# Six 32-byte tiles moved ahead of the weight region in SBUF: every tile of that region, with two gain tiles and a table tile, lies 192 bytes higher

## The reference, cut to what matters

```python
h = rms_norm(x, norm_mix_pre)
z = h @ w_in                                  # 1024 x 1024 @ 1024 x 2816
a = window_attention(rope(aq), rope(ak), av, sink)   # band of +-128, 8 heads of 64
r = retention(rq, rk, rv, rg, ...)            # 4 heads of 128, two directions
x = x + rms_norm(concat(a, r) @ w_out, ...)   # @ 1024 x 1024
q = h2 @ xa_wq;  kv = mn @ xa_wkv             # 256 memory tokens
x = x + rms_norm(softmax(q k') v @ xa_wo, ...)
gate, up = split(h3 @ ffn_w_gu)               # @ 1024 x 5632
x = x + rms_norm((silu(gate) * up) @ ffn_w_down, ...)
```

## Time and profile before

| | |
|---|---|
| median of 3 runs | 1387.6 us (1385.53 to 1387.71) |
| span of the profiled execution, first to last instruction | 1384.9 us |
| TensorE busy | 1364.0 us, 98% of the span, 6644 matmuls |
| weight loads (PEld) busy | 1136.0 us, 82% |
| VectorE, ScalarE, GpSimd busy | 878.7, 671.2, 882.7 us |
| granted clock of TensorE, mean | 1.000 |
| chain that ended last | PE 80%, DVE 8%, ACT 4%, POOL 3%, issue 2%, DMA 2% |

### The profile page before, as it was taken

One profiled execution on the slowest core, in us unless ns is written; L12 is line 12 of the kernel. 1 busy time (PEld: TensorE's weight loads), 2 busy tenths in 40 slices (PEclk: granted clock), 3 DMA queues, 4 the chain that ended last, 5 costly groups with the idle time before them and its releaser, 6 DMA issues.

```text
span 1384.9 us, 18822 instructions
## 1 busy us (share of the span) xinstructions
PE 1364.0 (98%) x6644; PEld 1136.0 (82%) x6644; DVE 878.7 (63%) x1230; ACT 671.2 (48%) x1357; POOL 882.7 (64%) x624
## 2 busy tenths in 40 slices
PE   7999999999999999999999999999999999999998
PEld 7998888767988888888888788888888888878886
DVE  5799997787987788764278732233333334574878
ACT  6432233677686774354386433333333333534454
POOL 1697256335778976512355788777777773799653
PEclk9999999999999999999999999999999999999999
DMA  5676133332028554301535233333333225933354
GB/s 205 208 251 208 53 92 93 106 122 93 1 62 304 182 179 152 101 26 39 190 124 182 88 102 100 107 100 114 114 103 109 97 81 199 355 96 96 115 203 153
DMA packets 137756, 183.56 MB, mean 133 GB/s; under 512 B 10304, under 2 KB 82368, under 8 KB 137664
## 3 DMA queue, kind: packets, MB, share of 16 engines
q1 hardware_dynamic: 135360, 177.25, 38.7%
q10 hardware_dynamic: 2304, 5.13, 1.0%
HBM read 136.98 MB, written 45.35 MB: 132 GB/s over the span
## 4 chain that ended last, share of the span: by engine, by line
PE 80%; DVE 8%; ACT 4%; POOL 3%; issue 2%; DMA 2%; SPq 0%; DVEq 0%; ACTq 0%; POOLq 0%
PE ps L1407 23%; PE ps L1409 23%; PE ps L1408 23%; PE ps L1398 4%; PE ps L1921 2%; PE ps L1619 1%; PE ps L1581 1%; POOL w_lo L1276 1%; DMA raw<-in_xa_wkv_dram 1%; PE ps L1673 1%; ACT tables L2132 1%; DVE x L3807 1%; DMA raw<-o_sums 1%; DVE left_a L3751 1%; DVE yf L3800 1%
## 5 line engine op out<-in xcount | busy, mean ns | idle before, releaser
L1407 PE MATMUL ps<-w_hi,t_hi 128*128 128x512 f32 (+2 forms) x576 | 219.4, 381 | 2.2 <-DVE t_lo L3026 1.2
L1409 PE MATMUL ps<-w_hi,t_lo 128*128 128x512 f32 (+2 forms) x576 | 217.6, 378 | 0.0
L1408 PE MATMUL ps<-w_lo,t_hi 128*128 128x512 f32 (+2 forms) x576 | 217.4, 377 | 0.0
L1138 POOL TENSOR_TENSOR w_lo<-raw,w_hi 128x512 fp32r<-128x512 f32 (+1 forms) x52 | 82.9, 1601 | 95.6 <-ACT w_hi L2185 95.4
L1407 PEld LDWEIGHTS ps<-w_hi,t_hi 128*128 128x128 f32 x576 | 108.2, 188 | 20.3 <-DVE t_lo L3026 1.6
L1409 PEld LDWEIGHTS ps<-w_hi,t_lo 128*128 128x128 f32 x576 | 108.2, 188 | 17.7
L1408 PEld LDWEIGHTS ps<-w_lo,t_hi 128*128 128x128 f32 x576 | 108.3, 188 | 17.1
L1292 POOL TENSOR_TENSOR w_lo<-raw,w_hi 128x512 fp32r<-128x512 f32 x32 | 42.0, 1322 | 96.9 <-ACT w_hi L2663 96.9
L3709 DVE TENSOR_TENSOR ev<-ps,ev 128x512 f32<-128x512 f32 x21 | 14.5, 691 | 135.1 <-PE ps L1409 135.1
L2853 ACT ACTIVATE ev<-ps 128x512 f32<-128x512 f32 x63 | 37.4, 594 | 86.1 <-PE ps L1409 86.1
L2185 ACT ACTIVATE w_hi<-raw 128x512 fp32r<-128x512 f32 (+1 forms) x52 | 31.4, 616 | 97.1 <-PE ps L1409 96.8
(11 more groups left out here) (391 smaller groups left out, 4114.4 us busy)
## 6 DMA issues: line engine op xcount, KB each, us to landing
raw_a<-in_ffn_w_gu_dram SPq DMA_DIRECT2D x44, 256.0 KB, 3.2
raw_b<-in_ffn_w_gu_dram SPq DMA_DIRECT2D x44, 256.0 KB, 3.2
f_rows<-fs SPq DMA_DIRECT2D x44, 256.0 KB, 3.7
gain_b<-f_rows SPq DMA_DIRECT2D x39, 256.0 KB, 2.8
tables<-f_rows SPq DMA_DIRECT2D x38, 256.0 KB, 2.7
f_rows<-fa SPq DMA_DIRECT2D x33, 256.0 KB, 3.5
raw<-in_xa_wo_dram SPq DMA_DIRECT2D x32, 256.0 KB, 2.6
wd_rest<-in_ffn_w_down_dram SPq DMA_DIRECT2D x15, 512.0 KB, 7.3
```

Of the source, the lines that this page charges most:

```text
L1138: nc.gpsimd.tensor_tensor(w_lo[:, k, 0:width], raw[:, k, 0:width], w_hi[:, k, 0:width].bitcast(F32), ALU.subtract).then_inc(w_split, 1)
L1407: nc.tensor.matmul(out, a_hi, b_hi, start=start, stop=False, skip_group_check=onto)
L1408: nc.tensor.matmul(out, a_hi, b_lo, start=False, stop=False, skip_group_check=onto)
L1409: return nc.tensor.matmul(out, a_lo, b_hi, start=False, stop=stop, skip_group_check=onto)
```

## The change

```diff
         dec_t = sb("dec_t", [P, 3, 2 * RH])
 
+        sink_in = sb("sink_in", [P, AH])
+        sink = sb("sink", [P, AH])
+        nsink = sb("nsink", [P, AH])
+        dec = sb("dec", [P, 2 * RH])
+        lg = sb("lg", [P, 2 * RH])
+        cdec = sb("cdec", [P, 2 * RH])
+
         R = overlay(
...
         gain_a = sb("gain_a", [P, D])
         gain_b = sb("gain_b", [P, D])
-        sink_in = sb("sink_in", [P, AH])
-        sink = sb("sink", [P, AH])
-        nsink = sb("nsink", [P, AH])
-        dec = sb("dec", [P, 2 * RH])
-        lg = sb("lg", [P, 2 * RH])
-        cdec = sb("cdec", [P, 2 * RH])
         vpow = sb("vpow", [P, 2 * RH])
```

## The result

The changed kernel takes 1396.56 us (median of 4 runs, 1394.09 to 1397.62), the one before 1387.44 (4 runs, 1385.53 to 1387.71). The ratio is 1.0067, 95% interval 1.0054 to 1.0079: slower by 9 us, where no change was forecast. (The time still lies inside the stated range, in the part that a slower rival had brought in.)

A forecast was written before the change was run, and what follows sets the result against it. TensorE was taken as the bound, busy 1364.0 of 1384.9 us. The terms summed to 0, so the span stayed at 1384.9 us; with the runs' median 2.7 us above, the forecast was 1387.6 us, range 1370 to 1398.

The forecast's parts named there:

- slower rival: TensorE's shifted pairs run at 230.0 ns: 2340 x 3.3 ns = +7.7 us, 1395.3 us; slower had chance 0.26.
- Step (b): TensorE's 2340 matmuls with one operand shifted against the other, 1752 with the stream 64 bytes below, 588 above: price 0.
- faster end: Lower bound on the price of TensorE's shifted matmuls: 2340 x -10.6 ns = -24.8 us.
- slower end: Upper bound for TensorE's shifted matmuls, at the worst single unsettled step, 0.24 us: 2340 x 13.3 ns = +31.1 us.
- the unsettled stretch: TensorE's starts behind a wait: eleven distances from 378.59 to 381.12 us, 230.0 ns each, before 226.7 is reached.
- The down product is not among them: Down product's matmuls not counted as shifted: `right_a` and `left_a` move together, `right_b` and `left_b` not at all.
- (a): The six small tiles, read in short set-up operations and as per-partition scalars, keep size and form: 0.
- (c): DMAs into the shifted tiles, whose rows may now begin on a multiple of 256: taken as 0, under 1 us.
- (d): VectorE, ScalarE and GpSimd on shifted tiles: taken as 0; a tenth on four GpSimd subtractions would be 0.9 us.
- The faster side: Shifted matmuls gain: half of its chance near 1374.7 us, the rest split between 1382.5 and 1367.1; chance 0.36.
- the half-and-half case: Opposite signs of shift on TensorE: 1752 matmuls could gain and 588 lose; counted with the faster ones.
- 0.228 or more: Sign of the slower side: start-to-start distance in us in the input projection, with the down product as before.

The follow-up runs named there:

- e12: `w_hi` and `w_lo` made parts of one tile, beginning 4 bytes into it, against the kernel before: 1400.56 us, ratio 1.0099.
- e9: Three small tiles put ahead of the weight region (+96 bytes), against the kernel before: 1401.77 us, ratio 1.0112.
- e8: `raw`, `wz`, `right_a` and `left_a` shifted as in the change, `w_hi` and `w_lo` back at distance 0, against the kernel before: 1387.80 us, ratio 1.0012.
- e1: All eight small tiles put ahead of the weight region, which lies 256 bytes higher, against the kernel before: 1386.46 us, ratio 0.9996.
- e2: `zero` and `eps` moved to the very end, so everything behind `ident` lies 64 bytes lower together, against the kernel before: 1386.36 us, ratio 0.9995.
- e3: Two small tiles put ahead of the weight region (+64 bytes), against the kernel before: 1394.19 us, ratio 1.0052.
- e10: Five small tiles put ahead of the weight region (+160 bytes, that is -96), against the kernel before: 1402.55 us, ratio 1.0117.
- e7: Six small tiles put between `w_hi` and `w_lo`, so of TensorE's operands `w_lo` alone is shifted, against the kernel before: 1390.88 us, ratio 1.0034.
- e5: One small tile put ahead of the weight region (+32 bytes), against the kernel before: 1400.74 us, ratio 1.0107.

## Why the prediction was wrong, step by step

**Step (b), the price of a shifted matmul, failed.** It was taken as 0 and bounded from -10.6 to +13.3 ns. With every instruction, wait and transfer alike, the pace goes from 226.7 ns to as much as 236.7 (e12) by the distance of the two operands. The runs put +6.6 ns in its place for the stream at -64 (1464 of them at 512 columns, somewhat less where a stage restarts often), +2.2 for the stream at +64 (588), -1.6 for 416 columns (192) and 0 for 352 (96). The counts were right, and the prices measured lie between the ends. The reason for the 0 was not right: that "the rhythm comes back to it after a disturbance" was seen among pairs at distance 0 alone, and says nothing on where the rhythm settles for a pair at another distance. The prediction had noted that the trace held no other pair, and then took the sameness of four stages as evidence about one. What varied between those stages was everything but the thing that the change varies.

**No run shows the -10.6 ns of the faster end.** No distance brought the pace of the float32r matmuls of 512 columns below 226.7 ns. The 216 ns of plain fp32, which the expectation of e9 still sets beside them, come from the earlier trace rows and are off by a factor of two as a price for a matmul. There 21 records span 4.70 us; less the last one's own 0.38 and over 20 that is 216.0 ns from start to start. But the code issues 64 matmuls of 256 columns for these scores, and the trace has 128 records of them. So 216.0 ns is the time of a record, half a matmul, and a whole one takes 432; it says nothing on what a float32r matmul of 512 columns could gain. These records keep their 216.0 ns in all layouts, but `kM` and `qX` lie in one region, so no run changed their distance. Of the slower end, +13.3 ns, the step of 0.24 us is 236 ns before rounding (the starts lie at 379.051 and 379.287 us), so it should have been +9.3; e12's streamed weights run at such a step throughout, 236.7 ns, although no row of the trace before kept one for two matmuls.

**The slower rival had the right sign and the right kind of effect**: a rhythm that settles at a longer pace, of which it took the unsettled stretch as the model. It said +3.3 ns for all 2340, +7.7 us, 1395.3; measured were 11 us of TensorE and 9 us of span, 1396.6. It mis-sized the two directions as one (6.6 and 2.2; (1464 x 6.6 + 588 x 2.2 - 192 x 1.6) / 2340 = 4.6 on the mean). That its time came out so near is luck: it had too small a price for a matmul, and the span grew by 2 us less than the matmuls did. It was given 0.26, the least of the three.

**"The down product is not among them" was wrong in part.** Its own pairs were at distance 0, as said, but at each change from pair a to pair b one load of `left_b` runs under a stream of `right_a` (e8). What matters there is the operand loaded next, not only the matmul's own. The pace of `right_a` went from 226.8 to 227.3 ns, that of `right_b` from 226.9 to 228.6, about 1.0 us in all. In the profile shorter waits ahead of `right_b` hide it, waits that e1 has too.

**(a), (c) and (d) at 0 held**: e2 moves them all and measures 0.9995. The memory's part, through which the chain of the earlier trace rows runs by GpSimd and DMA, did not grow (-0.7 us, within what its wait varies by). The output projection has no such cover: with attention it grew by 2.4 us, and both rows begin behind it, at 462.81 us and later.

**The faster side**, given 0.36, fell with every run. Its values, 1374.7, 1382.5 and 1367.1 us, rest on a gain for each matmul that no run shows: 64 bytes shorten the 226.7 ns of distance 0 in neither direction (233.3 at -64, 228.9 at +64), and e3 (ratio 1.0052) closes the half-and-half case, in which one direction gains. The only gain clear of the scatter is that of 416 columns.

Of what the prediction wanted to look at, the pace of the input projection ("0.228 or more") was the sign that told; `wz` and the input projection parted company as it said they might.

Open: why distance 0 is best, and by which rule the pace follows the distance; no run here shows a mechanism. Open too is what the pace at distance 0 is made of. From 352 columns (160.0 ns) to 512 (226.7) it grows by 0.417 ns a column; by that slope 512 columns take 213.3 ns and about 13.3 are left. That is an estimate from these two paces alone, and the 188.3 ns of 416 columns lie 1.7 above its line. Nor was a distance other than 0 tried with the tokens at another place.

## What to carry to other kernels

This kernel is bound by matmuls of float32r parts, 512 columns wide, with a new stationary operand each time (6644 loads for 6644 matmuls), and in it a small tile allocated between two large ones was an edit to TensorE's pace, up to 1.2% of the time (e10): 226.7 ns at distances of 0 and 256 bytes, 228.8 to 236.7 at all others tried. On a kernel like it, keep every pair of streamed and next loaded operand at the same place modulo 256, and put odd-sized small tiles behind them all, in sets that add up to 256 bytes. Look for it in the distances between starts over a hundred matmuls, not in the mean length of a group. And when the trace holds one value of the thing that a change varies, an even pace across everything else is no evidence that the thing is free.

## What the hardware showed that was not expected

The pace of these matmuls depends on the distance of their operands (226.7 ns at 0, up to 236.7 in e12), is not monotonic in it (32 bytes cost 6.6 ns, +64 only 2.2, +96 again 6.6), and has a sign: exchanging which operand streams exchanges the paces, at 64 (233.3 and 228.8 ns in the change, 228.9 and 233.3 in e3) and at 96 (233.3 and 234.2 in e9, 234.2 and 233.3 in e10). It has a memory: one crossing pair slowed the twelve matmuls behind it by 3.3 ns each (e8), and a third of shifted products slowed all three alike (e7, 229.2, 229.3 and 228.4 ns). It depends on the number of columns: -64 costs 6.6 ns at 512 columns, nothing at 352 (the half of them that is shifted), and gains 1.6 at 416, where e5 (+32) costs 4.9. A shift by 64 bytes did not touch the plain fp32 transposes of 128 columns (e2, 109.2 and 109.1 ns); for wider plain fp32 matmuls no run tried it.
